# Log weights of key block 0 in stick-breaking attention: a sum over all key blocks, corrected by a triangle

## The chip, the cores and the metric

The kernel runs on one core of one Trainium2 chip. The metric is the device time of one execution in microseconds (us), and 0.2% of it is 3.8 us. The engines are named as the profile names them: PE is TensorE (PEld its weight loads), DVE is VectorE, ACT is ScalarE, POOL is GpSimd and SP is SyncE, which issues the loads.

## The reference, cut to what matters

Two transformer blocks are computed on 512 rows plus 16 meta rows, width 1024. Only the stick-breaking attention of the first block concerns this change: 16 heads of width 64.

```python
z = jnp.einsum('bhtd,bhsd->bhts', q_blk, k_pre) * scale
valid = (s_pos[None, :] < t_pos[:, None]) & (s_pos[None, :] >= PAD)
log_not = jnp.where(valid, jax.nn.log_sigmoid(-z), 0.0)
after = lax.cumsum(log_not, axis=3, reverse=True) - log_not
a = jnp.where(valid, jnp.exp(jax.nn.log_sigmoid(z) + after), 0.0)
outs.append(jnp.einsum('bhts,bhse->bhte', a, v_pre))
```

With sp = softplus(z) the log of a weight is z minus the sum of sp over this key and all later keys that the query may see. So each head needs, for each key, a reversed running sum of sp over the keys.

## The kernel before

**Tiling.** Scores are held transposed: keys on the 128 partitions, queries along the columns. The 512 keys are four key blocks. Block 0 is seen by all 512 queries, block 1 by the last 384, block 2 by 256, block 3 by 128; they are packed in `sp` at the columns `KEY_OFF`, 1280 in all. In PSUM block 0 fills bank 4, block 1 bank 5, blocks 2 and 3 share bank 6. Bank 7 holds the scores of the meta keys. Every fp32 product is made of split values: an x_hi in fp32r and the rest x_lo, so that a running sum over sp is two matmuls, one with `sp_hi` and one with `sp_lo`.

**One head** (its number is g, four heads to a quad, two heads to a pair p):

- `scores` on PE writes z into banks 4 to 6.
- `softplus` on ACT and DVE makes sp: Abs, Exp, Ln on ACT, then the maximum is added on DVE (steps sp1, sp2, sp0), ACT writes `sp_hi` (hi1 for blocks 1 to 3, hi0 for block 0), DVE `sp_lo` (sp_lo1, sp_lo0). Then DVE adds blocks 1 to 3 onto block 0, one after another, in place (L1507, steps all1 to all3): `sp[:, 0:SEQ]` is then the sum of all blocks.
- `logs` on PE subtracts the running sums from z in PSUM, by a product with a constant matrix from `cmat`: `C_TRI` (minus one on and below the diagonal) for a block onto itself, `C_ALL` (all minus one) for a later block onto an earlier one. It goes by the target block 1, 2, 3 and then 0. `logs1` is signalled after block 3, `logs0` after block 0.
- `weights` on ACT and DVE: ACT writes `sp_all_hi` (all_hi) from the sum of all blocks, DVE `sp_all_lo` (all_lo, L1512); then ACT takes Exp of the logs (a_part1, a_part2, a_part0) and the hi parts, DVE the lo parts `a_lo`.
- `meta_logs` on PE uses `sp_all_hi` and `sp_all_lo` for the meta keys, one product pair for each head, after `meta_softplus` has prepared them for both heads of the pair.
- `outputs` on PE multiplies the weights with the values.

**What sets the order.** There is no scheduler. Each engine has its own list of instructions, written by hand in a function `quad_body` per engine, and the engines meet at semaphores: `Steps` gives each step of a head a count, in the fixed order of its list. Each queue runs in order, so an instruction that waits holds all behind it. On PE the steps of one head are laced with strips of projections, which are to cover ACT and DVE: `logs(g)` stands behind the first value strip, `logs(g + 1)` behind a key strip, `logs(g + 2)` behind half of a projection, `logs(g + 3)` behind the next key strip. In quads 2 to 4 the half before `logs(g + 2)` is four strips of a "D" unit, whose results DVE adds into `acc` (L1589); strips 6 and 7 of these are added by DVE inside `softplus(g + 2)`, between sp_lo0 and the adds of L1507. In the first quad DVE copies one strip into `logit` (L1605) at that place. A strip's PSUM bank is used again two strips later, once DVE has signalled `strip_free`. In the last quad no key strip follows, and a shorter projection stands before `logs(g + 3)`.

ACT and DVE also split each 2048-column unit of weights (`split_hi`, `split_lo`), which stand in their lists between these steps.

Of the kernel before, what the change touches and what calls it, by code (L numbers as in the profile page):

```python
# [34 lines left out]
SEQ = 512  # L35
# [4 lines left out]
MROWS = 4 * META  # L40
# [131 lines left out]
def build(nc, units, xfm, meta2, consts, dec, vecs, out):  # L172
# [355 lines left out]
    def _(pe):  # L528
# [146 lines left out]

        def logs(g):

            for b in (1, 2, 3, 0):
                pe.wait_ge(hd_dve.sem, hd_dve.at("sp_lo1" if b else "sp_lo0", g))
                for b2 in range(b, BLOCKS):  # L680
                    c0 = KEY_COL[b] + P * (b2 - b)
                    for x in (sp_hi, sp_lo):
                        m = nc.tensor.matmul(psum[:, 4 + KEY_BANK[b], c0:c0 + KEY_LEN[b2]],  # L683
                                             cmat[:, C_TRI if b2 == b else C_ALL, :],
                                             x[:, KEY_OFF[b2]:KEY_OFF[b2] + KEY_LEN[b2]],
                                             start=False, stop=False, skip_group_check=True)
                if b in (3, 0):
                    m.then_inc(*hd_pe.step("logs1" if b else "logs0"))

        def meta_scores(t, p):  # L690

# [4 lines left out]
        def meta_logs(r, p, g):  # L696

            if r == 0:
                pe.wait_ge(mk_dve.sem, mk_dve.at("m_lo", p))
                for x in (m_hi, m_lo):  # L700
                    nc.tensor.matmul(psum[0:MROWS, 7, :], cmat[:, C_TRI_META, 0:MROWS], x[:, :], start=False,
                                     stop=False, skip_group_check=True)
            pe.wait_ge(hd_dve.sem, hd_dve.at("all_lo", g))
            for x in (sp_all_hi, sp_all_lo):
                m = nc.tensor.matmul(psum[0:MROWS, 7, :], cmat[:, C_ROWS + r, 0:MROWS], x[:, :], start=False,
                                     stop=False, skip_group_check=True)
            if r == 1:
                m.then_inc(*mk_pe.step("m_rows"))
# [250 lines left out]
    def _(act):  # L959
        def a(out_, in_, f, **kw):  # L960
            return nc.scalar.activation(out_, in_, f, **kw)  # L961
# [82 lines left out]
                act.wait_ge(hd_dve.sem, hd_dve.at(ready, g))  # L1044
                a(sp_hi[:, cols], sp[:, cols], ACT.Copy).then_inc(*hd_act.step(f"hi{n}"))

        def weights(g):

            act.wait_ge(hd_dve.sem, hd_dve.at("all3", g))
            a(sp_all_hi[:, :], sp[:, 0:SEQ], ACT.Copy).then_inc(*hd_act.step("all_hi"))  # L1050
            for half, cols, parts in ((1, H1, (1, 2)), (0, H0, (0,))):
                act.wait_ge(hd_pe.sem, hd_pe.at(f"logs{half}", g))
                for n in parts:
                    bank, off, w = PARTS[n]
                    a(a_f[:, off:off + w], psum[:, 4 + bank, 0:w], ACT.Exp).then_inc(*hd_act.step(f"a_part{n}"))
                act.wait_ge(hd_act.sem, hd_act.at(f"a_part{parts[-1]}", g))
                a(a_hi[:, cols], a_f[:, cols], ACT.Copy).then_inc(*hd_act.step(f"a_hi{half}"))

        def meta_softplus(p):
            act.wait_ge(mk_pe.sem, mk_pe.at("m_scores", p))  # L1060
            a(m_f[0:MROWS, :], psum[0:MROWS, 7, :], ACT.Abs).then_inc(*mk_act.step("m_abs"))
            act.wait_ge(mk_act.sem, mk_act.at("m_abs", p))
            a(m_f[0:MROWS, :], m_f[0:MROWS, :], ACT.Exp, scale=-1.0).then_inc(*mk_act.step("m_exp"))
            act.wait_ge(mk_act.sem, mk_act.at("m_exp", p))
            a(m_f[0:MROWS, :], m_f[0:MROWS, :], ACT.Ln, bias=g_col("one", 0)[0:MROWS]).then_inc(*mk_act.step("m_ln"))
            act.wait_ge(mk_dve.sem, mk_dve.at("m_sp", p))
            a(m_hi[0:MROWS, :], m_f[0:MROWS, :], ACT.Copy).then_inc(*mk_act.step("m_hi"))

# [31 lines left out]
        def quad_body(at, i, has_d, has_next):  # L1100
            g, p = 4 * i, 2 * i
            nj, ns = 3, 12 if has_d else 6
            softplus(g)
            meta_softplus(p)
            if has_d:
                y_hi(1, p - 1)
            value_hi(at, 0)
            weights(g)
            value_hi(at, 1)
            split_hi(at, 0)  # L1110
            softplus(g + 1)
            key_hi(1, at, 2, p + 1)
            weights(g + 1)
            query_hi(1, at, 3)
            meta_weights(p)
            softplus(g + 2)
            split_hi(at, 1)
            meta_softplus(p + 1)
            weights(g + 2)
            strips(at, ns - 1)  # L1120
            split_hi(at, 2)
            y_hi(0, p)
            softplus(g + 3)
# [285 lines left out]
    def _(dve):  # L1409
# [97 lines left out]
                v.tensor_tensor(sp[:, b * P:SEQ], sp[:, b * P:SEQ], sp[:, KEY_OFF[b]:KEY_OFF[b] + KEY_LEN[b]],  # L1507
                                ALU.add).then_inc(*hd_dve.step(f"all{b}"))

        def weights(g):  # L1510
            dve.wait_ge(hd_act.sem, hd_act.at("all_hi", g))
            v.tensor_tensor(sp_all_lo[:, :], sp[:, 0:SEQ], as_f32(sp_all_hi[:, :]), ALU.subtract)\  # L1512
                .then_inc(*hd_dve.step("all_lo"))
            for half, cols in ((1, slice(SEQ, PACKED)), (0, slice(0, SEQ))):
                dve.wait_ge(hd_act.sem, hd_act.at(f"a_hi{half}", g))
                v.tensor_tensor(a_lo[:, cols], a_f[:, cols], as_f32(a_hi[:, cols]), ALU.subtract)\
                    .then_inc(*hd_dve.step(f"a_lo{half}"))

        def meta_softplus(p):
            dve.wait_ge(mk_act.sem, mk_act.at("m_ln", p))  # L1520
            stt(m_f[0:MROWS, :], psum[0:MROWS, 7, :], 0.0, m_f[0:MROWS, :], ALU.max, ALU.add).then_inc(*mk_dve.step("m_sp"))
            dve.wait_ge(mk_act.sem, mk_act.at("m_hi", p))
            v.tensor_tensor(m_lo[0:MROWS, :], m_f[0:MROWS, :], as_f32(m_hi[0:MROWS, :]), ALU.subtract).then_inc(*mk_dve.step("m_lo"))

# [74 lines left out]
        def quad_body(at, i, has_d, has_next):  # L1599
            g, p = 4 * i, 2 * i  # L1600
            nj, ns = 3, 12 if has_d else 6

            def take_logit(n, s):
                strips(at, s)
                v.tensor_copy(logit[:, n, :], strip_view(at.bank(s), SEQ)).then_inc(strip_free, 1)  # L1605
            softplus(g)
            meta_softplus(p)
            if has_d:
                y_lo(1, p - 1)
            value_lo(at, 0, i)  # L1610
            weights(g)
            value_lo(at, 1, i)
            split_lo(at, 0)
            softplus(g + 1)
            key_lo(1, at, 2, p + 1)
            weights(g + 1)
            query_lo(1, at, 3, p + 1)
            meta_weights(p)
            y_take(p)
            softplus(g + 2, has_d and (lambda: add_up(acc, at, 4, range(2))),  # L1620
                     (lambda: add_up(acc, at, 6, range(2, 4))) if has_d else (lambda: take_logit(0, 4)))
            meta_softplus(p + 1)
# [433 lines left out]
def constants():  # L2058
# [10 lines left out]
    cm[:, C_BLOCKED] = np.where(i[:, None] < i[None, :], 0.0, BLOCKED)  # L2069
    cm[:, C_TRI] = np.where(i[:, None] >= i[None, :], -1.0, 0.0)  # L2070
    cm[:, C_ALL] = -1.0
    same = (i[:, None] < 2 * META) & (head[:, None] == head[None, :])
    cm[:, C_TRI_META] = np.where(same & (i[:, None] % META >= i[None, :] % META), -1.0, 0.0)
    for j in range(2):
        cm[:, C_ROWS + j] = np.where(head[None, :] == j, -1.0, 0.0)
# [100 lines left out]
```

## Time and profile before

| what | value |
|---|---|
| median of 3 runs | 1903.82 us (1903.22 to 1905.71) |
| the profiled execution | 1905.67 us, span in the trace 1903.9 us |
| PE busy | 1852.1 us, 97% |
| DVE busy, ACT busy | 1115.6 us, 731.1 us |
| the chain that ended last | PE 87%, DVE 6%, ACT 3% |
| the four quads | about 35 to 366 us of the span |

The page gives busy times and the chain that ended last. A timeline lists the instructions of an engine in order of time with start and duration. A matmul's duration holds its way through the array, so that consecutive matmuls overlap in it: what one costs PE is the distance between two starts. An idle note in brackets stands where the engine had nothing running, and names what ended it.

### The profile page before, as it was taken

To read this page: it belongs to the slowest core of one execution; us is meant where nothing else is said; L and a number is where in the kernel's file an instruction comes from. 1 tells how busy PE (TensorE), PEld (TensorE's weight loads), DVE (VectorE), ACT (ScalarE), POOL (GpSimd) and SP (SyncE) were. 2 spreads that over 40 slices of the span, in tenths; PEclk is the share of its full clock that TensorE was granted. 3 is DMA by queue.
4 is the path that set the end of the run, shared out by engine and by line. 5 is a ranking of instruction groups with operands and counts; after the bars stand their busy time and mean duration, and the time that the engine had idled before them with its cause. 6 is when DMAs were issued, how large, how long until landed. Compare 5 with 4: busy or idle time off the path is not lost.

```text
span 1903.9 us, 24558 instructions
## 1 busy us (share of the span) xinstructions
PE 1852.1 (97%) x9844; PEld 1585.1 (83%) x9844; DVE 1115.6 (59%) x1423; ACT 731.1 (38%) x868; POOL 32.6 (2%) x32
## 2 busy tenths in 40 slices
PE   9999999999999999999899999999999899999996
PEld 8898989789898888988788888886997688888885
DVE  6567566653635537356565454547688565454546
ACT  5666666433323332333342222224445542222222
POOL 2000000010000000000000000000000000000000
PEclk9999999999999999999999999999999899999998
DMA  4011111132122221112413223222467212322221
GB/s 180 28 69 60 44 44 45 45 122 78 67 88 77 88 99 66 67 67 74 195 45 108 91 88 108 90 90 87 111 177 181 108 45 89 109 89 90 108 90 45
DMA packets 24770, 168.98 MB, mean 89 GB/s; under 512 B 2688, under 2 KB 2944, under 8 KB 5248
## 3 DMA queue, kind: packets, MB, share of 16 engines
q1 hardware_dynamic: 23120, 156.51, 23.1%
q0 software_dynamic: 1584, 11.54, 2.9%
q8 instruction: 48, 0.79, 0.2%
q14 instruction: 18, 0.15, 0.0%
HBM read 154.40 MB, written 2.10 MB: 82 GB/s over the span
## 4 chain that ended last, share of the span: by engine, by line
PE 87%; DVE 6%; ACT 3%; issue 2%; DMA 1%; SPq 0%; DVEq 0%; ACTq 0%; POOL 0%; POOLq 0%
PE psum L531 28%; PE psum L532 27%; PE psum L533 27%; PE psum L683 2%; ACT w_hi L961 1%; PE psum L640 1%; DVE normed L1422 1%; DMA w_raw<-in_units 1%; DVE h L1449 1%; PE psum L611 1%; DVE w_lo L1416 1%; PE psum L593 0%; DVE normed L1466 0%; PE psum L601 0%; ACT std L961 0%
## 5 line engine op out<-in xcount | busy, mean ns | idle before, releaser
L531 PE MATMUL psum<-X_hi,w_hi 128*128 128x512 f32 (+1 forms) x1632 | 588.3, 360 | 3.1 <-DVE w_lo L1416 2.2
L532 PE MATMUL psum<-X_lo,w_hi 128*128 128x512 f32 (+1 forms) x1632 | 581.9, 357 | 0.0
L533 PE MATMUL psum<-X_hi,w_lo 128*128 128x512 f32 (+1 forms) x1632 | 581.9, 357 | 0.0
L961 ACT ACTIVATE w_hi<-w_raw 128x2048 fp32r<-128x2048 f32 x134 | 255.8, 1909 | 372.0 <-PE psum L533 364.7
L1416 DVE TENSOR_TENSOR w_lo<-w_raw,w_hi 128x2048 fp32r<-128x2048 f32 x123 | 281.7, 2290 | 135.5 <-ACT w_hi L961 135.5
L531 PEld LDWEIGHTS psum<-X_hi,w_hi 128*128 128x128 f32 x1632 | 306.8, 188 | 51.6 <-issue 4.2
L532 PEld LDWEIGHTS psum<-X_lo,w_hi 128*128 128x128 f32 x1632 | 307.4, 188 | 46.0 <-issue 2.4
L533 PEld LDWEIGHTS psum<-X_hi,w_lo 128*128 128x128 f32 x1632 | 307.0, 188 | 44.2
L1589 DVE TENSOR_TENSOR acc<-acc,psum 128x512 f32<-128x512 f32 x216 | 141.9, 684 | 59.9 <-PE psum L533 59.5
L531 PE MATMUL psum<-M_hi,w_hi 128*128 128x512 f32 x352 | 136.9, 389 | 0.0
L532 PE MATMUL psum<-M_lo,w_hi 128*128 128x512 f32 x352 | 136.9, 389 | 0.0
L533 PE MATMUL psum<-M_hi,w_lo 128*128 128x512 f32 x352 | 136.9, 389 | 0.0
L531 PE MATMUL psum<-w_hi,X_hi 128*128 128x256 f32 x384 | 108.8, 283 | 0.0
L532 PE MATMUL psum<-w_lo,X_hi 128*128 128x256 f32 x384 | 108.7, 283 | 0.0
L533 PE MATMUL psum<-w_hi,X_lo 128*128 128x256 f32 x384 | 108.6, 283 | 0.0
L1870 DVE TENSOR_TENSOR gate_in<-psum,std 128x512 f32<-128x512 f32 x44 | 30.2, 691 | 122.1 <-PE psum L533 109.0
L961 ACT ACTIVATE silu_a<-gate_in 128x512 f32<-128x512 f32 x44 | 27.6, 631 | 168.9 <-DVE gate_in L1870 168.9
L1422 DVE SCALAR_TENSOR_TENSOR z<-glu,vec,z 128x512 f32<-128x512 f32 x120 | 80.3, 746 | 0.0
L533 PEld LDWEIGHTS psum<-M_hi,w_lo 128*128 128x128 f32 x352 | 66.1, 188 | 13.7
L531 PEld LDWEIGHTS psum<-M_hi,w_hi 128*128 128x128 f32 x352 | 66.1, 188 | 13.7
L532 PEld LDWEIGHTS psum<-M_lo,w_hi 128*128 128x128 f32 x352 | 66.1, 188 | 13.7
L531 PEld LDWEIGHTS psum<-w_hi,X_hi 128*128 128x128 f32 x384 | 73.6, 192 | 0.9
(282 smaller groups left out, 2644.2 us busy)
## 6 DMA issues: line engine op xcount, KB each, us to landing
w_raw<-in_units SPq DMA_DIRECT2D x140, 1024.0 KB, 4.8
w_lo<-w_raw POOLq DMA_DIRECT2D x11, 1024.0 KB, 6.9
h<-in_xfm SPq DMA_DIRECT2D x4, 528.0 KB, 6.2
h<-in_xfm SPq DMA_DIRECT2D x1, 2112.0 KB, 7.4
decay<-in_dec SPq DMA_DIRECT2D x4, 512.0 KB, 4.4
out<-h SPq DMA_DIRECT2D x4, 512.0 KB, 2.8
rot<-in_consts SPq DMA_DIRECT2D x1, 528.0 KB, 12.3
acc<-in_consts SPq DMA_DIRECT2D x1, 448.0 KB, 10.0
```

What stands on the lines that cost most here:

```text
L531: nc.tensor.matmul(dst, w2[0], x2[0], start=first, stop=False, skip_group_check=True)
L532: nc.tensor.matmul(dst, w2[0], x2[1], start=False, stop=False, skip_group_check=True)
L533: m = nc.tensor.matmul(dst, w2[1], x2[0], start=False, stop=last, skip_group_check=True)
L611: nc.tensor.matmul(psum[:, bank, 0:P], ones[:, :], ones[:, :], start=True, stop=True)
L640: m = nc.tensor.matmul(psum[0:rows, at.bank(s) + 1, 0:256], XM[:, k, meta], y[:, k, :], start=k == 0 and y is w[0], stop=k == DT - 1 and y ...
L683: m = nc.tensor.matmul(psum[:, 4 + KEY_BANK[b], c0:c0 + KEY_LEN[b2]], cmat[:, C_TRI if b2 == b else C_ALL, :], x[:, KEY_OFF[b2]:KEY_OFF[b2 ...
L961: return nc.scalar.activation(out_, in_, f, **kw)
L1416: v.tensor_tensor(lo, w_raw[at.ring(j)][:, :], as_f32(hi), ALU.subtract).then_inc(w_lo_ready, 1)
L1422: return v.scalar_tensor_tensor(out=out_, in0=in0, scalar=scalar, in1=in1, op0=op0, op1=op1)
L1449: v.tensor_tensor(h[:, k, META:FULL], h[:, k, META:FULL], normed[:, k % 2, 0:SEQ], ALU.add)\
L1589: v.tensor_tensor(dst[:, m, :], dst[:, m, :], strip_view(at.bank(s + n), SEQ), ALU.add)\
L1870: v.tensor_tensor(gate_in[:, c, :], strip_view(at.bank(s + c), SEQ), std[:, 0:SEQ], ALU.mult)\
```

## The change

Four things are done.

1. `logs(g)` on PE first makes the blocks 1 to 3 as before. For block 0 it then makes, in place of four pairs of matmuls (512, 384, 256 and 128 columns), two pairs of 512 columns: `C_ABOVE` (one above the diagonal, else zero) with `sp_hi`, `sp_lo` of block 0, and `C_ALL` (minus one everywhere) with `sp_all_hi`, `sp_all_lo`. Minus all of block 0 plus what lies above the diagonal is the triangle; the later blocks are in the sum. The second pair waits for all_lo.
2. all_hi leaves ACT's `weights` and becomes `added_hi`; all_lo leaves DVE's `weights` and becomes `added_lo`. In the heads g + 1 and g + 3 they are called right behind `softplus`, before `key_hi` and `key_lo`. In the heads g and g + 2 they are called inside `meta_softplus`: on ACT between m_ln and m_hi, on DVE between m_sp and m_lo.
3. On ACT `meta_softplus(p + 1)` is moved ahead of `split_hi(at, 1)`.
4. The two 64-column matrices `C_ROWS` share one slot of `cmat`, which makes room for `C_ABOVE`.

The diff, cut:

```diff
         def logs(g):
-            for b in (1, 2, 3, 0):
-                pe.wait_ge(hd_dve.sem, hd_dve.at("sp_lo1" if b else "sp_lo0", g))
+            pe.wait_ge(hd_dve.sem, hd_dve.at("sp_lo1", g))
+            for b in range(1, BLOCKS):
                 for b2 in range(b, BLOCKS):
...
-                if b in (3, 0):
-                    m.then_inc(*hd_pe.step("logs1" if b else "logs0"))
+            m.then_inc(*hd_pe.step("logs1"))
+
+            pe.wait_ge(hd_dve.sem, hd_dve.at("sp_lo0", g))
+            for x in (sp_hi, sp_lo):
+                nc.tensor.matmul(psum[:, 4, :], cmat[:, C_ABOVE, :], x[:, 0:SEQ], start=False, stop=False,
+                                 skip_group_check=True)
+            pe.wait_ge(hd_dve.sem, hd_dve.at("all_lo", g))
+            for x in (sp_all_hi, sp_all_lo):
+                m = nc.tensor.matmul(psum[:, 4, :], cmat[:, C_ALL, :], x[:, :], start=False, stop=False,
+                                     skip_group_check=True)
+            m.then_inc(*hd_pe.step("logs0"))
...
-        def weights(g):
-
+        def added_hi(g):
             act.wait_ge(hd_dve.sem, hd_dve.at("all3", g))
             a(sp_all_hi[:, :], sp[:, 0:SEQ], ACT.Copy).then_inc(*hd_act.step("all_hi"))
+
+        def weights(g):
...
-        def meta_softplus(p):
+        def meta_softplus(p, then):
...
             a(m_f[0:MROWS, :], m_f[0:MROWS, :], ACT.Ln, bias=g_col("one", 0)[0:MROWS]).then_inc(*mk_act.step("m_ln"))
+            then()
             act.wait_ge(mk_dve.sem, mk_dve.at("m_sp", p))
...
             softplus(g + 2)
+            meta_softplus(p + 1, lambda: added_hi(g + 2))
             split_hi(at, 1)
-            meta_softplus(p + 1)
             weights(g + 2)
...
-        def weights(g):
+        def added_lo(g):
             dve.wait_ge(hd_act.sem, hd_act.at("all_hi", g))
             v.tensor_tensor(sp_all_lo[:, :], sp[:, 0:SEQ], as_f32(sp_all_hi[:, :]), ALU.subtract)\
                 .then_inc(*hd_dve.step("all_lo"))
```

In the loop of the quads, head g + 2, on DVE before: the second of the adds of strips 6 and 7 (`acc`), the three adds of all blocks (`sp<-sp`), the meta part, strips 8 and 9, a unit of weights, and only then `sp_all_lo`.

```order
L1589 TENSOR_TENSOR acc<-acc,psum 128x512
L1506 ISA
L1507 TENSOR_TENSOR sp<-sp 128x384
...
L1507 TENSOR_TENSOR sp<-sp 128x128
L1520 ISA
L1422 SCALAR_TENSOR_TENSOR m_f<-psum,m_f 64x512
L1522 REGISTER_ALU
L1523 TENSOR_TENSOR m_lo<-m_f,m_hi 64x512
...
L1416 TENSOR_TENSOR w_lo<-w_raw,w_hi 128x2048
L1511 REGISTER_ALU
L1512 TENSOR_TENSOR sp_all_lo<-sp,sp_all_hi 128x512
```

The same place on DVE after the change:

```order
L1605 TENSOR_TENSOR acc<-acc,psum 128x512
L1519 ISA
L1520 TENSOR_TENSOR sp<-sp 128x384
...
L1520 TENSOR_TENSOR sp<-sp 128x128
L1535 ISA
L1435 SCALAR_TENSOR_TENSOR m_f<-psum,m_f 64x512
L1524 REGISTER_ALU
L1525 TENSOR_TENSOR sp_all_lo<-sp,sp_all_hi 128x512
L1538 REGISTER_ALU
L1539 TENSOR_TENSOR m_lo<-m_f,m_hi 64x512
```

`sp_all_lo` moved ahead of `m_lo`, of two strip additions and of the unit's `w_lo`; the two strip additions and the three adds still stand before it.

On ACT, at the same head of the first quad (`w_hi` is `split_hi`, the first `a_f` is a_part1), before:

```order
L961 ACTIVATE sp_hi<-sp 128x512
L961 ACTIVATE w_hi<-w_raw 128x2048
L961 ACTIVATE m_f<-psum 64x512
L961 ACTIVATE m_f<-m_f 64x512
L961 ACTIVATE m_f<-m_f,vec 64x512
L961 ACTIVATE m_hi<-m_f 64x512
L961 ACTIVATE sp_all_hi<-sp 128x512
L961 ACTIVATE a_f<-psum 128x384 x2
```

and after:

```order
L970 ACTIVATE sp_hi<-sp 128x512
L970 ACTIVATE m_f<-psum 64x512
L970 ACTIVATE m_f<-m_f 64x512
L970 ACTIVATE m_f<-m_f,vec 64x512
L970 ACTIVATE sp_all_hi<-sp 128x512
L970 ACTIVATE m_hi<-m_f 64x512
L970 ACTIVATE w_hi<-w_raw 128x2048
L970 ACTIVATE a_f<-psum 128x384 x2
```

The unit's `w_hi` moved from the front of the meta part to its end, and `sp_all_hi` ahead of `m_hi`.

## Rows read from the trace of the kernel before

**Rows 1.** Page, part 1: busy us, share of the span, instructions.

```profile
PE 1852.1 (97%) x9844; PEld 1585.1 (83%) x9844; DVE 1115.6 (59%) x1423; ACT 731.1 (38%) x868; POOL 32.6 (2%) x32
```

**Rows 2.** PE waits, 28 to 375 us: total us, times, longest.

```profile
...
PE psum L531 <- DVE Q_lo L1422: 2.4, 1, 2.4
...
```

**Rows 3.** Timeline (start, duration us, instruction, idle): PE, head g+2, second quad.

```profile
169.62 0.45 PE L683 MATMUL psum<-sp_hi,cmat 128*128 128x512 f32 x1
...
170.89 0.45 PE L531 MATMUL psum<-Y_hi,w_hi 128*128 128x512 f32 x1
...
173.49 0.39 PE L533 MATMUL psum<-Y_hi,w_lo 128*128 128x512 f32 x1
174.01 0.50 PE L531 MATMUL psum<-Y_hi,w_hi 128*128 128x512 f32 x1
...
176.90 0.40 PE L701 MATMUL psum<-m_hi,cmat 128*64 128x512 f32 x1
...
177.46 0.45 PE L705 MATMUL psum<-sp_all_hi,cmat 128*64 128x512 f32 x1
...
177.99 0.39 PE L531 MATMUL psum<-Q_hi,K_hi 128*128 128x512 f32 x1
```

**Rows 4.** Timeline, DVE, same head (xN: N instructions merged).

```profile
168.55 1.28 DVE L1589 TENSOR_TENSOR acc<-acc,psum 128x512 f32<-128x512 f32 x2
169.74 1.33 DVE L1507 TENSOR_TENSOR sp<-sp 128x384 f32<-128x384 f32 x3
171.29 0.68 DVE L1422 SCALAR_TENSOR_TENSOR m_f<-psum,m_f 64x512 f32<-64x512 f32 x1 [0.22 <-ACT m_f L961]
...
176.72 0.69 DVE L1512 TENSOR_TENSOR sp_all_lo<-sp,sp_all_hi 128x512 fp32r<-128x512 f32 x1
```

**Rows 5.** Timeline, ACT, the same head.

```profile
167.46 1.90 ACT L961 ACTIVATE w_hi<-w_raw 128x2048 fp32r<-128x2048 f32 x1
169.26 0.57 ACT L961 ACTIVATE m_f<-psum 64x512 f32<-64x512 f32 x1
...
170.53 0.72 ACT L961 ACTIVATE m_f<-m_f,vec 64x512 f32<-64x512 f32 x1
...
172.54 0.61 ACT L961 ACTIVATE sp_all_hi<-sp 128x512 fp32r<-128x512 f32 x1
```

**Rows 6.** Timeline, head g+2 of the first quad, DVE and PE.

```profile
86.38 1.33 DVE L1507 TENSOR_TENSOR sp<-sp 128x384 f32<-128x384 f32 x3
...
88.28 0.45 PE L531 MATMUL psum<-X_hi,w_hi 128*128 128x512 f32 x1
```

**Rows 7.** Timeline, head g+1 of the second quad, DVE and PE.

```profile
146.57 1.35 DVE L1507 TENSOR_TENSOR sp<-sp 128x384 f32<-128x384 f32 x3
...
148.63 0.44 PE L683 MATMUL psum<-sp_hi,cmat 128*128 128x512 f32 x1
...
149.90 0.45 PE L531 MATMUL psum<-X_hi,w_hi 128*128 128x512 f32 x1
```

**Rows 8.** Timeline, head g of the first quad, DVE and PE.

```profile
44.37 1.34 DVE L1507 TENSOR_TENSOR sp<-sp 128x384 f32<-128x384 f32 x3
...
46.88 0.44 PE L683 MATMUL psum<-sp_hi,cmat 128*128 128x512 f32 x1
```

**Rows 9.** Timeline, head g+3 of the last quad, DVE and PE.

```profile
355.97 0.69 DVE L1512 TENSOR_TENSOR sp_all_lo<-sp,sp_all_hi 128x512 fp32r<-128x512 f32 x1
...
356.87 0.45 PE L531 MATMUL psum<-X_hi,w_hi 128*128 128x512 f32 x1
```

**Rows 10.** Timeline, PE, first product after the quads.

```profile
369.64 0.80 PE L531 MATMUL psum<-Y_hi,w_hi 128*128 128x512 f32 x1 [3.58 <-DVE Y_lo L1538]
...
374.92 0.40 PE L531 MATMUL psum<-Y_hi,w_hi 128*128 128x512 f32 x1
```

**Rows 11.** Windows: us, busy PE PEld DVE ACT POOL, PEclk, DMA share, GB/s.

```profile
33.00:36.00 3.00, 1.21 (x6) 1.10 (x7) 2.78 (x6) 2.40 (x2) 2.71 (x6) 1.00 0.79 295
...
369.00:372.00 3.00, 2.36 (x6) 1.89 (x7) 0.58 (x1) 0.00 (x0) 0.00 (x0) 0.50 0.00 0
```

More of the change, by code:

```diff
@@ L704, in meta_logs @@
             for x in (sp_all_hi, sp_all_lo):
-                m = nc.tensor.matmul(psum[0:MROWS, 7, :], cmat[:, C_ROWS + r, 0:MROWS], x[:, :], start=False,
+                m = nc.tensor.matmul(psum[0:MROWS, 7, :], cmat[:, C_ROWS, MROWS * r:MROWS * (r + 1)], x[:, :], start=False,
                                      stop=False, skip_group_check=True)
@@ L1103, in quad_body @@
             softplus(g)
-            meta_softplus(p)
+            meta_softplus(p, lambda: added_hi(g))
             if has_d:
@@ L1111, in quad_body @@
             softplus(g + 1)
+            added_hi(g + 1)
             key_hi(1, at, 2, p + 1)
@@ L1123, in quad_body @@
             softplus(g + 3)
+            added_hi(g + 3)
             if has_next:
@@ L1513, in weights @@
                 .then_inc(*hd_dve.step("all_lo"))
+        def weights(g):
             for half, cols in ((1, slice(SEQ, PACKED)), (0, slice(0, SEQ))):
@@ L1517, in weights, with meta_softplus @@
                     .then_inc(*hd_dve.step(f"a_lo{half}"))
-        def meta_softplus(p):
+        def meta_softplus(p, then):
             dve.wait_ge(mk_act.sem, mk_act.at("m_ln", p))
             stt(m_f[0:MROWS, :], psum[0:MROWS, 7, :], 0.0, m_f[0:MROWS, :], ALU.max, ALU.add).then_inc(*mk_dve.step("m_sp"))
+            then()
             dve.wait_ge(mk_act.sem, mk_act.at("m_hi", p))
@@ L1606, in quad_body @@
             softplus(g)
-            meta_softplus(p)
+            meta_softplus(p, lambda: added_lo(g))
             if has_d:
@@ L1614, in quad_body @@
             softplus(g + 1)
+            added_lo(g + 1)
             key_lo(1, at, 2, p + 1)
@@ L1621, in quad_body @@
                      (lambda: add_up(acc, at, 6, range(2, 4))) if has_d else (lambda: take_logit(0, 4)))
-            meta_softplus(p + 1)
+            meta_softplus(p + 1, lambda: added_lo(g + 2))
             if has_d:
@@ L1633, in quad_body @@
             softplus(g + 3)
+            added_lo(g + 3)
             if has_next:
@@ L2040, in z_done @@
     return 2 * TAPS_B * (t // 2) + 2 * TAPS_B - 1 + t % 2
-C_IDENT, C_BLOCKED, C_TRI, C_ALL, C_TRI_META, C_ROWS = 0, 1, 2, 3, 4, 5
+C_IDENT, C_BLOCKED, C_TRI, C_ALL, C_TRI_META, C_ROWS, C_ABOVE = range(7)
 N_CMAT = 7
@@ L2071, in constants @@
     cm[:, C_ALL] = -1.0
+    cm[:, C_ABOVE] = np.where(i[:, None] >= i[None, :], 0.0, 1.0)
     same = (i[:, None] < 2 * META) & (head[:, None] == head[None, :])
@@ L2074, in constants @@
     for j in range(2):
-        cm[:, C_ROWS + j] = np.where(head[None, :] == j, -1.0, 0.0)
+        cm[:, C_ROWS, MROWS * j:MROWS * (j + 1)] = np.where(head[None, 0:MROWS] == j, -1.0, 0.0)
     consts = np.concatenate([cos, sin, cm.reshape(P, -1)], axis=1).astype(np.float32)
```

## The prediction

> **What bounds the kernel now.** The first view is the page's busy time of the engines: PE works for 97% of the span [rows 1], so a microsecond taken from PE is won only if nothing else becomes late, and one microsecond in which PE stands still is lost whole. The next is the timeline of PE inside the quads. The reader is to see there the distance between two starts: from 170.89 to 173.49 eleven matmuls of 512 columns start [rows 3], 0.236 us each. Then the timelines of DVE and ACT around the same head tell when the sum of all blocks is there, since PE is to wait for it now. PE, DVE and ACT are all laid out by hand, so each of the four places of `logs` in a quad is looked at by itself.
>
> **What the change saves on PE.** Before, block 0 took from 169.62 to 170.89 [rows 3], 1.27 us for 2560 columns; the heads in other places show the same 1.27 (148.63 to 149.90) [rows 7]. After, it is two pairs of 512 columns, each pair behind a wait. The pair behind a wait that the trace has is that of L705: 177.46 to 177.99, 0.53 us [rows 3]. Two such pairs are 1.06 us, so a head saves 0.21 us if PE never stands, and sixteen heads 3.4 us.
>
> **What the new wait costs.** The sum of all blocks needs, behind the third add of L1507: all_hi on ACT, 0.61 us [rows 5], and all_lo on DVE, 0.69 us [rows 4]. A hand-over costs about 0.05 us: PE started at 177.46, all_lo had ended at 176.72 + 0.69 = 177.41 [rows 3, 4]. I take 0.05 for each of the three hand-overs. So PE can start the second pair 0.05 + 0.61 + 0.05 + 0.69 + 0.05 = 1.45 us after the third add ends. Now place by place.
>
> *Head g.* In the first quad the adds end at 44.37 + 1.34 = 45.71, so all_lo reaches PE at 47.16; the first pair runs from 46.88 to 47.41 [rows 8]. There is 0.25 us to spare, since a whole value strip stood in between. The later quads have more, their value strip being no shorter. Net -0.21 us, four times: -0.8 us. Behind it, m_hi on ACT moves back by almost nothing, because it waits for m_sp anyway.
>
> *Head g + 1.* The adds end at 146.57 + 1.35 = 147.92, PE may go on at 149.37; the first pair ends at 148.63 + 0.53 = 149.16. PE stands 0.21 us, and then needs 0.53 us: 149.90, which is the very time at which the next strip started before [rows 7]. The saving is eaten: 0.0 us, in all four quads. On ACT `key_hi` now stands behind all_hi, and on DVE `key_lo` behind all_lo, but their keys are needed only after another half projection and the outputs of a head; that hides it, and without this cover it would cost the 0.6 us (all_hi) by which they move.
>
> *Head g + 3* has the same order in quads 1 to 3, so again 0.0 us. In the last quad PE comes there sooner, because a projection of 512 columns stands in place of the key strip of 528. all_lo ended at 355.97 + 0.69 = 356.66 already as early as it can; PE goes on at 356.71 and is through at 357.24, against 356.87 before [rows 9]: +0.4 us.
>
> *Head g + 2* is where the sum stands or falls. On DVE the adds of L1507 stand behind two strip additions, which begin at 168.55 and end at 169.83; the three adds then end at 169.74 + 1.33 = 171.07 [rows 4]. PE may start the second pair at 172.52. But its first pair is through at 169.62 + 0.53 = 170.15 [rows 3]: PE stands 2.4 us. m_sp does not make it worse: on ACT the meta steps took from 169.26 to 171.25, 1.99 us, and moved ahead of the unit's `w_hi` they run from 167.46 to 169.45 [rows 5], so m_sp (0.68) follows the third add directly and ends about when all_hi does [rows 4]. PE is through at 173.05, against 170.89: +2.16 us.
>
> Two small waits of before then go. Strip 10 waited for its bank, since DVE came late to strip 8: 173.49 to 174.01 is 0.52 where 0.236 is usual, and the restart shows 0.50 for 0.39, together 0.39 us [rows 3]. With PE 2.2 us later, DVE is ahead of it again. And L705 waited for all_lo: the two pairs from 176.90 to 177.99 took 0.56 + 0.53 where four starts of 0.236 are 0.94, 0.15 us [rows 3]. So +2.16 - 0.39 - 0.15 = +1.6 us for quads 2, 3 and 4. What is queued behind: on ACT the unit's `w_hi` (1.90 us) now runs after m_hi, about 172.4 to 174.3, so a_part1 starts some 1.2 us later than before, at 173.15 [rows 5]; on DVE the strip additions and the unit's `w_lo` follow PE. All their users on PE stand 1.6 us or more later, so they meet the same cover. The load that SP issues behind this unit slips by about 2 us; its data are used two heads later.
>
> In the first quad only one strip copy stands there and the adds end at 86.38 + 1.33 = 87.71; PE goes on at 89.16 and is through at 89.69, against 88.28 before [rows 6]: +1.4 us, with no small waits to win back.
>
> **The sum.** Head g: -0.8. Heads g + 1 and g + 3: 0.0 and +0.4. Head g + 2: 1.4 + 3 x 1.6 = +6.2. Together +5.8 us. The profiled execution has a span of 1903.9 us and a device time of 1905.67, 1.8 us more; it becomes 1909.7 and 1911.5. The median of the runs is 1903.82, and I forecast 1903.8 + 5.8 = 1909.6 us, 0.3% slower.
>
> **Bounds.** The hand-overs are the softest term: at 0.03 in place of 0.05 each of twelve or so stalls is 0.06 shorter, -0.7 us; at 0.08 it is 0.09 longer, +1.1. After the last quad PE idles 3.58 us anyway, and then runs at half its clock: twelve matmuls from 369.64 to 374.92 took 5.28 us where 2.83 is usual, 2.45 us lost [rows 10]. How long that stretch is depends on the moment at which the clock changes, and the times of before differ among themselves by as much, 1903.22 to 1905.71. A shift of the whole program can move this by some 1.5 us in either direction.
>
> **The rivals.**
>
> *The cold clock.* PE stands 2.4 us at four places. Against this rival: a wait of 2.4 us for Q_lo near 35 us [rows 2] left the clock at 1.00 in the stretch around it; for it: after 3.58 us of idle time it was at 0.50, 1.2 GHz [rows 10, 11]. If it fell at one to four of these places, each would cost the 2.45 us of above: 1912 to 1919 us. The Trainium skill (TensorE: Matmul & The Clock Gate, "What's actually happening") states that the fast clock is held by activity and that an idle TensorE is taken back to half; by that rule the change would be worse than my sum, and the trace agrees for the long wait, not for the one of 2.4 us.
>
> *The other side: the sum is there in time.* If all_lo reached PE before it had finished the first pair, in all sixteen heads, only the saving were left: 3.4 us of PE time and three times the 0.15, 1903.8 - 3.9 = 1899.9 us, faster. It speaks for it that heads g do just this. It decides at head g + 2: the chain there must become 2.4 us shorter for the full gain, and 1.4 us shorter for no change. I see nothing that shortens it: DVE's queue has the strip additions ahead of the adds, and these wait for strips which PE finishes right before `logs`.
>
> *Only half of it shows.* The stalls come as computed, but the cold stretch behind the quads, or those around the norms, fall more favourably by up to 2.45 us, and the hand-overs are at their lower end: 1909.6 - 2.45 - 0.7 = 1906.4 us, which is inside 0.2% of before.
>
> *A later step goes late:* weights or scores of head g + 3 wait for ACT because `w_hi` moved. The cover there is the scores that PE does in between; without any of it, the 1.2 us by which a_part1 moves would be paid in three quads, 1909.6 + 3.6 = 1913.2 us.
>
> **How the numbers follow.** The forecast of 1909.6 with its own bounds (1907.7 to 1912) has 0.68; the half effect 0.14; the cold clock 0.09; the late step 0.04; the sum in time 0.05. What a measurement of this kernel can tell from no change is about 0.2%, 3.8 us. Faster by more than that is the rival in time, 0.05. Within it lie the half effect and a little of the forecast's lower edge, 0.17. Slower: 0.78. For eight times in ten the range runs from 1906.2, the half effect's end, to 1912.5, which leaves out the cold clock and the rival in time.
>
> **What would show it.** In the timeline of PE, L695 must start some 2.4 us after L691 is through at head g + 2 of every quad (about 2.0 us idle in the first, 2.2 in the others), 0.2 us after it at g + 1 and g + 3, with no idle note at g. The waits of PE must name `sp_all_lo` with some 9 us in total, and the waits for L1512 before L705 must be gone. The distance from `logs(g)` of quad 2 to that of quad 3 must grow by 1.6 - 0.2 = 1.4 us. If the chain of DVE and ACT behind the third add is much longer or shorter than 1.45 us, the size is wrong; if PEclk falls inside the quads, the first rival is right; if L695 never waits at g + 2, the forecast is wrong as a whole.

## The result, and the profile after

The changed kernel takes 1912.35 us in the median of 7 runs (1911.53 to 1917.93), the kernel before 1905.34 in as many (1903.22 to 1906.67). The ratio is 1.0041, with a 95% interval of 1.0032 to 1.0050: slower by some 7 to 8 us, where 5.8 had been forecast. The profiled execution has a span of 1910.0 us, 6.1 more than before.

PE does less work, as it should: 1849.8 us busy with 64 instructions fewer, against 1852.1 us [rows 1]. From part 1 of the page of the changed kernel:

```profile
PE 1849.8 (97%) x9780; PEld 1579.1 (83%) x9780; DVE 1115.4 (58%) x1423; ACT 730.8 (38%) x868; POOL 32.6 (2%) x32
```

What it waits for from 28 to 382 us (total us, times, longest) has a new first line, the wait of the second pair (L695) for the lower part of the sum of all blocks:

```profile
PE psum L695 <- DVE sp_all_lo L1525: 8.5, 5, 2.2
PE psum L531 <- DVE Y_lo L1554: 3.6, 1, 3.6
```

The place is head g + 2. PE in the second quad, in the changed kernel (L691 is the triangle pair, L695 the pair with the sum):

```profile
169.72 0.44 PE L691 MATMUL psum<-sp_hi,cmat 128*128 128x512 f32 x1
170.00 0.40 PE L691 MATMUL psum<-sp_lo,cmat 128*128 128x512 f32 x1
172.60 0.76 PE L695 MATMUL psum<-sp_all_hi,cmat 128*128 128x512 f32 x1 [2.20 <-DVE sp_all_lo L1525]
173.16 0.63 PE L695 MATMUL psum<-sp_all_lo,cmat 128*128 128x512 f32 x1
173.58 0.63 PE L531 MATMUL psum<-Y_hi,w_hi 128*128 128x512 f32 x1
...
175.29 0.63 PE L532 MATMUL psum<-Y_lo,w_hi 128*128 128x512 f32 x1
175.72 0.57 PE L533 MATMUL psum<-Y_hi,w_lo 128*128 128x512 f32 x1
176.12 0.40 PE L531 MATMUL psum<-Y_hi,w_hi 128*128 128x512 f32 x1
```

The idle time of 2.20 us is what was forecast, and so is the chain that causes it. The same instruction in quads 1, 3 and 4:

```profile
88.33 0.50 PE L695 MATMUL psum<-sp_all_hi,cmat 128*128 128x512 f32 x1 [1.46 <-DVE sp_all_lo L1525]
258.52 0.80 PE L695 MATMUL psum<-sp_all_hi,cmat 128*128 128x512 f32 x1 [2.22 <-DVE sp_all_lo L1525]
344.13 0.50 PE L695 MATMUL psum<-sp_all_hi,cmat 128*128 128x512 f32 x1 [2.20 <-DVE sp_all_lo L1525]
```

The fifth wait of 8.5 us is the 0.44 us at head g + 3 of quad 4. DVE and ACT at head g + 2 of the second quad:

```profile
169.82 1.34 DVE L1520 TENSOR_TENSOR sp<-sp 128x384 f32<-128x384 f32 x3
171.07 0.68 DVE L1435 SCALAR_TENSOR_TENSOR m_f<-psum,m_f 64x512 f32<-64x512 f32 x1
171.85 0.69 DVE L1525 TENSOR_TENSOR sp_all_lo<-sp,sp_all_hi 128x512 fp32r<-128x512 f32 x1
```

```profile
171.19 0.63 ACT L970 ACTIVATE sp_all_hi<-sp 128x512 fp32r<-128x512 f32 x1 [1.66 <-DVE sp L1520]
```

From the end of the third add, 169.82 + 1.34 = 171.16, to the start of L695 at 172.60 are 1.44 us; 1.45 were computed from [rows 3 to 5]. But look at the durations behind the wait. A matmul of 512 columns lasts 0.63 us there and the next starts 0.43 us later, where 0.40 and 0.236 are usual; from 176.12 on it is usual again. The granted clock of these stretches (us, busy of PE, PEld, DVE, ACT, POOL, PEclk, DMA share, GB/s), in the changed kernel:

```profile
170.00:173.00 3.00, 0.80 (x3) 0.40 (x2) 2.83 (x6) 1.81 (x3) 0.00 (x0) 0.94 0.00 0
173.00:176.00 3.00, 3.00 (x8) 2.35 (x8) 0.14 (x1) 2.97 (x5) 0.00 (x0) 0.50 0.00 0
176.00:179.00 3.00, 3.00 (x14) 2.38 (x14) 1.97 (x3) 0.95 (x2) 0.00 (x0) 0.99 0.00 0
...
258.00:261.00 3.00, 2.48 (x6) 2.02 (x7) 1.06 (x2) 2.97 (x5) 0.00 (x0) 0.50 0.00 0
...
343.00:346.00 3.00, 1.87 (x8) 1.57 (x9) 1.57 (x3) 3.00 (x4) 0.00 (x0) 1.00 0.00 0
```

So behind the stall the clock was at 0.50, 1.2 GHz. The same happened in quad 3 (258 to 261 us). In quads 1 and 4 it stayed at 1.00; the last line is the stretch behind the stall of quad 4, equally long (2.20 us idle).

To tell place from place, the distance from the first matmul of one head's `logs` to that of the next is taken from the timelines of PE. Everything else in the program is outside of these columns.

| us from `logs` to `logs` | before | after | difference |
|---|---|---|---|
| g to g + 1, quads 1 to 4 | 20.29, 20.38, 20.38, 20.30 | 19.96, 20.02, 20.02, 19.94 | -1.4 |
| g + 1 to g + 2 | 19.83, 20.90, 20.90, 20.90 | 19.75, 20.85, 20.83, 20.86 | -0.2 |
| g + 2 to g + 3 | 19.29, 20.03, 20.03, 19.66 | 20.67, 23.21, 22.93, 21.22 | +9.0 |
| g + 3 to the next g, quads 1 to 3 | 21.94 three times | 21.88, 21.86, 21.88 | -0.2 |
| g + 3 of quad 4 to the last product | 15.48 | 15.81 | +0.3 |
| ahead of the first, and behind the last | 45.45, 1534.2 | 45.03, 1533.3 | -1.4 |

The sum is +6.1 us, the difference of the spans. The last row has none of the changed work in it. Of its 1.4 us 0.4 stand ahead of the first `logs`, and 0.8 behind the wait for Y_lo, where the stretch at 1.2 GHz was shorter this time: the first twelve matmuls took 5.28 us in the kernel before [rows 10] and 4.44 after. Profiles of the same kernel differ there too: ahead of the first `logs` e1_again below has 46.32 us where this one has 45.03. Inside the quads the change cost 7.5 us.

### The profile page after: what moved, and what is told of

It is laid out like the page before. It is cut to its first block, busy times and chain, and to the rows that moved or that the text cites. A ratio compares the mean times of both kernels' runs of the same rounds, so it can differ in the third digit from the quotient of the medians.

```text
span 1910.0 us, 24430 instructions
## 1 busy us (share of the span) xinstructions
PE 1849.8 (97%) x9780; PEld 1579.1 (83%) x9780; DVE 1115.4 (58%) x1423; ACT 730.8 (38%) x868; POOL 32.6 (2%) x32
## 4 chain that ended last, share of the span: by engine, by line
PE 83%; DVE 8%; ACT 5%; issue 3%; DMA 1%; POOL 0%; DVEq 0%; SPq 0%; ACTq 0%; POOLq 0%
PE psum L531 26%; PE psum L532 26%; PE psum L533 26%; PE psum L640 1%; ACT sp L970 1%; DVE normed L1435 1%; ACT w_hi L970 1%; DVE sp L1520 1%; DMA w_raw<-in_units 1%; DVE h L1462 1%; DVE sp_lo L1513 1%; PE psum L695 1%; DVE w_lo L1429 1%; DVE sp L1435 1%; ACT sp_hi L970 0%
```

## The experiments

The theory after this profile: the stall has its computed length, 2.2 us at head g + 2, and in some of its four places, by chance, the clock falls behind it, which costs another 1.6 us or so. The rival: the moved steps on ACT and DVE make something else late. All kernels below ran beside the kernel before, on three chips, where it took 1905.80 us (e1 to e4), 1905.59 (e5 to e8) and 1905.90 (e9 to e11); each ratio is to the kernel before on the same chip. Below, a slow stretch is one in which the granted clock is at 1.2 GHz.

**The changed kernel again**, twice (e1_again and e10_again2, on different occasions; no edit).

> The changed kernel once more, beside its variants. Theory (cold clock by chance): the stall at head g + 2 has the same length each time, 1.46 us in the first quad and 2.2 us in the others, but how many of the four are followed by a stretch at 1.2 GHz differs from run to run (two in the profiled run, 3.4 us each, about 1.6 us lost in each), so single times spread over several us, 1909 to 1918, about 7 us over before in the median. Rival (later step late): no spread beyond that of before, and the 7 us stand in places outside of head g + 2.

> The changed kernel once more, on the chip of e9_warm9 and e11_laced_filled. Theory: PE stands 2.2 us at head g + 2 of quads 2 to 4 as before, and two or three of the four places are followed by a stretch at 1.2 GHz, so about 7 us over before. Rival: no such stretch, and still 7 us.

1912.38 us (1911.29 to 1914.60) and 1912.02 us (1911.73 to 1915.04), ratios 1.0036 (1.0023 to 1.0050) and 1.0039 (1.0026 to 1.0053). From `logs(g + 2)` to `logs(g + 3)` the profile of e1_again has 22.26, 23.19, 22.94 and 21.22 us, that of e10_again2 20.68, 23.15, 22.97 and 21.26. So the first quad had a slow stretch in one of three profiles, quads 2 and 3 in all three, quad 4 in none. The single times lie in two groups, 1911.3 to 1912.4 and 1914.5 to 1917.9. The profile of e1_again, at 1914.60 us, is of the second group. Its span is 2.8 us longer than that of the first profile: 1.6 us at head g + 2 of quad 1, and 1.3 us ahead of the first `logs`, where another slow stretch stands (shown below, with the prediction). The idle times were the same in all three: 8.5 to 8.6 us in five waits. The rival falls, since the loss stands at head g + 2.

**A filler in the stall** (e2_warm). `keep_warm(n, 1)` makes n small matmuls of ones. On PE, between the two pairs of block 0:

```diff
+            keep_warm(warm, 1)
             pe.wait_ge(hd_dve.sem, hd_dve.at("all_lo", g))
...
-            logs(g + 2)
+            logs(g + 2, 16 if has_d else 10)
```

> The changed kernel with 16 small matmuls of ones (10 in the first quad) between the two pairs of block 0 at head g + 2, into a PSUM bank that is free there; they add no result. At the 0.115 us that such a one cost at the start of the kernel they fill 1.8 of the 2.4 us in which PE would stand. Theory (cold clock): the granted clock stays at 1.00 through the quads, each quad keeps its 2.2 us of delay but not the 1.6 us of a cold stretch, so this is 1 to 3 us faster than the changed kernel, about 1909.5, and its times spread no more than those of before. Rival (the 7 us are the stall and moved steps alone): the same time as the changed kernel.

1915.79 us (1912.87 to 1916.37), ratio 1.0049 (1.0036 to 1.0063): slower than e1_again, where 1 to 3 us faster had been expected. The clock did stay up in the quads, but the filler was too long. PE in the second quad of e2_warm:

```profile
171.77 0.39 PE L691 MATMUL psum<-sp_lo,cmat 128*128 128x512 f32 x1
172.00 3.73 PE L611 MATMUL psum<-ones 128*128 128x128 f32 x32
```

One fp32 matmul of ones makes two rows of 0.115 us, so sixteen are 32 rows and take 3.7 us, and 2.4 were to be filled. The distances are 21.18, 22.72, 22.75 and 22.36 us, 1.1 over what e9_warm9 shows below in quads 2 to 4. So the time of this run says nothing on the theory; what speaks for it is that no stretch in the quads was slow.

**The filler at the right length** (e9_warm9): nine and six in place of sixteen and ten.

> The changed kernel with a filler in the stall at head g + 2 as in e2_warm, but of 9 matmuls (6 in the first quad). In e2_warm each turned out as two rows of 0.115 us in the trace, 0.23 us, so that 16 took 3.7 us and reached over the stall; 9 take 2.1 us of the 2.4. Theory (cold clock): no stretch at 1.2 GHz behind the stalls, all_lo still sets the time of the second pair, and from logs(g + 2) to logs(g + 3) the quads take 20.7, 21.6, 21.6 and 21.2 us, as an undisturbed one did in the changed kernel: 1.5 to 4 us under the changed kernel beside it. Rival (the falls of the clock are not caused by these stalls): the same stretches at 1.2 GHz and the same time.

1910.29 us (1908.93 to 1910.80), ratio 1.0024 (1.0014 to 1.0034), against 1912.02 for e10_again2 beside it. The distances are 20.66, 21.63, 21.63 and 21.26 us; 20.7, 21.6, 21.6 and 21.2 had been expected. PE in the second quad and the granted clock behind it, in e9_warm9:

```profile
170.51 2.17 PE L611 MATMUL psum<-ones 128*128 128x128 f32 x18
172.89 0.50 PE L696 MATMUL psum<-sp_all_hi,cmat 128*128 128x512 f32 x1 [0.21 <-DVE sp_all_lo L1526]
173.22 0.40 PE L696 MATMUL psum<-sp_all_lo,cmat 128*128 128x512 f32 x1
173.46 0.39 PE L531 MATMUL psum<-Y_hi,w_hi 128*128 128x512 f32 x1
```

```profile
173.00:176.00 3.00, 3.00 (x13) 2.44 (x14) 1.11 (x2) 2.97 (x4) 0.00 (x0) 1.00 0.00 0
```

The second pair still starts when all_lo lands, so the delay itself is kept, and only the clock is different: 1.00 where it was 0.50. This parts the loss in two. The delay alone is 1.37 + 3 x 1.6 = 6.2 us in the four places. The slow stretches add 23.21 - 21.63 = 1.58 and 22.93 - 21.63 = 1.30 us in the profile of the changed kernel, which is 2.9 us together; in e10_again2, which ran beside e9_warm9, they add as much. The medians differ by only 1.7 us and the two spans by 1.8, because outside of the quads the profile of e9_warm9 took 1.0 us longer: 0.2 ahead of the first `logs` and 0.8 behind the wait for Y_lo. The ranges of the two kernels do not touch (to 1910.80, and from 1911.73).

**The old product at head g + 2 only** (e3_g2_old): `logs_old` is the function of before.

```diff
-            logs(g + 2)
+            logs_old(g + 2)
```

> The changed kernel, but at head g + 2 PE makes block 0 in the old way, from its own blocks, and does not wait for the sum. ACT and DVE stay in the new order. Theory: what remains is -0.8 us (heads g), 0.2 us for each head g + 1 and g + 3 as traced, +0.6 in the last quad, and -0.15 us three times: within 1 us of before, no cold stretch in the quads. Rival (the moved w_hi on ACT is what costs): still 4 us or more over before.

1902.47 us (1901.08 to 1903.41), ratio 0.9981 (0.9972 to 0.9990). The loss is gone, and the kernel is faster than before by more than had been expected. Its distances from g + 2 to g + 3 are 19.30, 19.57, 19.57 and 19.19 us, three of them 0.46 under before. The moved `w_hi` costs nothing: the rival falls.

**Only the moves on ACT and DVE** (e4_order_only): `logs_old` in all four places.

> Only the moves on ACT and DVE; PE makes the logs of block 0 in the old way in all heads. Theory: the moves cost nothing by themselves and take away the three waits of L705, so -0.5 us, no difference from before that can be told. Rival (the moves are what costs): several us over before, with PE waiting for a step that was on time.

1903.21 us (1900.68 to 1904.33), ratio 0.9986 (0.9977 to 0.9995), so 2.6 us under before, where 0.5 had been expected. The quads account for 1.4 of them: 19.59, 19.54 and 19.18 us from g + 2 to g + 3 of quads 2 to 4, where before has 20.03, 20.03 and 19.66. Strip 10 of the second quad no longer loses time with its bank. PE in e4_order_only:

```profile
173.25 0.39 PE L533 MATMUL psum<-Y_hi,w_lo 128*128 128x512 f32 x1
173.48 0.49 PE L531 MATMUL psum<-Y_hi,w_hi 128*128 128x512 f32 x1
```

The two starts are 0.23 us apart, where before has 0.52 [rows 3]. The meta steps now run ahead of `w_hi`, so DVE gets to strip 8 sooner. In the prediction these 0.39 us were won because PE came later; 0.29 of them are won by the order, stall or no stall (the restart still shows 0.49 us), and the 0.15 of L705 too, which makes the 0.44 to 0.49 us of a quad. The other 1.2 us of the median lie outside of the quads and inside the width of the interval.

**The new product at head g + 2 only** (e8_g2_only): `logs_old` at the other three.

> The new logs at head g + 2 alone; the other three heads make block 0 in the old way, with ACT and DVE in the new order. Theory: the whole loss is here, 1.4 + 3 x 1.6 us and the cold stretches, 6 to 9 us over before, no less than the changed kernel within 1 us. Rival (the loss is spread over the heads): under 4 us over before.

1912.10 us (1911.85 to 1916.01), ratio 1.0038 (1.0024 to 1.0051), 6.5 us over before: the whole loss is there. The distances are 20.68, 23.01, 21.59 and 24.08 us. This time the clock fell in quads 2 and 4, in the latter for longer, and quad 3 was spared: 21.59 is the undisturbed value of e9_warm9 within 0.04 us. The profile is that of the slowest run, 1916.01 us, so the long stretch of quad 4 is not typical of the median. The granted clock behind the stall of quad 4 in e8_g2_only:

```profile
344.00:347.00 3.00, 2.14 (x5) 1.75 (x6) 1.30 (x3) 3.00 (x5) 0.00 (x0) 0.54 0.03 5
347.00:350.00 3.00, 3.00 (x8) 2.32 (x8) 0.69 (x1) 2.19 (x4) 0.00 (x0) 0.50 0.00 0
```

So the same idle time is followed by a slow stretch at one place in one kernel and at another in the other. Whether that is chance, or follows from where in the program's time the stall falls, no run shows.

**A shorter chain** (e7_adds_first): on DVE strips 6 and 7 are added behind all_lo.

```diff
-            softplus(g + 2, has_d and (lambda: add_up(acc, at, 4, range(2))),
-                     (lambda: add_up(acc, at, 6, range(2, 4))) if has_d else (lambda: take_logit(0, 4)))
+            softplus(g + 2, has_d and (lambda: add_up(acc, at, 4, range(2))))
             meta_softplus(p + 1, lambda: added_lo(g + 2))
+            add_up(acc, at, 6, range(2, 4)) if has_d else take_logit(0, 4)
```

> The changed kernel, but on DVE the additions of strips 6 and 7 (the copy of the strip in the first quad) stand behind all_lo at head g + 2, so that the adds of all blocks follow sp_lo0 directly. Theory: the chain to all_lo is 1.2 us shorter (0.7 in the first quad), PE stands about 1.0 us in place of 2.2 at head g + 2, too short for the clock to fall; strips 8 and 9 wait a little for their banks, since strips 6 and 7 are freed later. 1905 to 1908, between before and the changed kernel. Rival: strips 8 and 9 wait as long as was won, 1910 or more.

1910.90 us (1909.72 to 1912.65), ratio 1.0028 (1.0017 to 1.0040): the expected range is missed, and the time is the rival's. PE and the granted clock in the last quad of e7_adds_first:

```profile
341.76 0.50 PE L695 MATMUL psum<-sp_all_hi,cmat 128*128 128x512 f32 x1 [1.14 <-DVE sp_all_lo L1522]
342.10 0.40 PE L695 MATMUL psum<-sp_all_lo,cmat 128*128 128x512 f32 x1
343.05 0.76 PE L531 MATMUL psum<-Y_hi,w_hi 128*128 128x512 f32 x1 [0.55 <-DVE acc L1602]
```

```profile
343.00:346.00 3.00, 2.95 (x7) 2.40 (x8) 0.52 (x2) 2.94 (x6) 0.00 (x0) 0.50 0.00 0
```

The stall is 1.14 us in place of 2.20, near the 1.0 computed, but strip 8 then waits 0.55 us for the bank that DVE frees later. The undisturbed second quad takes 21.28 us, only 0.35 under e9_warm9: of the 1.06 us by which the stall is shorter 0.7 are lost again. That is most of the rival's mechanism, though not all of what was won. The rest is the clock: quads 3 and 4, with two short waits close together, were followed by slow stretches and have 22.79 and 22.45 us, while quad 2, with the same two waits (1.15 and 0.46 us), was not.

**No wait at all** (e6_no_wait): the second pair reads `sp_hi` and `sp_lo`, which leaves the later blocks out of the sum.

```diff
-            pe.wait_ge(hd_dve.sem, hd_dve.at("all_lo", g))
-            for x in (sp_all_hi, sp_all_lo):
-                m = nc.tensor.matmul(psum[:, 4, :], cmat[:, C_ALL, :], x[:, :], start=False, stop=False,
+            for x in (sp_hi, sp_lo):
+                m = nc.tensor.matmul(psum[:, 4, :], cmat[:, C_ALL, :], x[:, 0:SEQ], start=False, stop=False,
```

> The changed kernel with the second pair of block 0 made from sp_hi and sp_lo of block 0 in place of the sum of all blocks, so that PE does not wait for all_lo; the later blocks are left out of the sum, so the logs of block 0 lack them. Theory: this is the price of the matmuls alone, 0.21 us less for a head and three waits of 0.15 gone, -3.9 us, 1901.5 where before is 1905.3. Rival (the pairs cost more than the trace of before shows): less than 2 us gained.

1899.15 us (1898.24 to 1900.62), ratio 0.9968 (0.9956 to 0.9980), 6.4 us under before. More is saved than expected. At heads g, g + 1 and g + 3 of quad 2 the distances are 20.02, 20.55 and 21.59 us, 0.35 under before each. A second pair whose wait is already met is cheap, as head g of the changed kernel shows, in the first quad:

```profile
46.98 0.40 PE L695 MATMUL psum<-sp_all_hi,cmat 128*128 128x512 f32 x1
47.22 0.39 PE L695 MATMUL psum<-sp_all_lo,cmat 128*128 128x512 f32 x1
47.44 0.28 PE L531 MATMUL psum<-w_hi,X_hi 128*128 128x256 f32 x1
```

The pair takes 0.46 us, no more than two matmuls in a row, and block 0 from 46.47 to 47.44 takes 0.97, not 1.06.

**The wait put where its data are ready** (e5_laced). The second pair leaves `logs` and becomes `logs_all`, which PE does among the matmuls of the projection behind it (`mid` calls a function ahead of the given one of the eight steps):

```diff
+        def logs_all(g):
             pe.wait_ge(hd_dve.sem, hd_dve.at("all_lo", g))
...
             logs(g)
+            logs_all(g)
...
-            unit(at, 1, 2, "P", SEQ, from_x, [1])
+            unit(at, 1, 2, "P", SEQ, from_x, [1], mid=(1, lambda: logs_all(g + 1)))
...
-                unit(at, dj, ds, "D", SEQ, y, range(4, 8))
+                unit(at, dj, ds, "D", SEQ, y, range(4, 6))
+                logs_all(g + 2)
+                unit(at, dj, ds, "D", SEQ, y, range(6, 8))
```

> The changed kernel, but on PE the pair with the sum of all blocks is taken out of logs and stands among the next projection: behind one of its eight steps at heads g + 1 and g + 3, behind strip 9 at head g + 2 (behind four of eight steps in the first quad). Theory: all_lo is there by then, PE never stands for it, and the saving of 0.2 us for a head is left, 16 x 0.21 + 0.45 = 3.9 us under before, about 1901.5 where before is 1905.3. Rival (a_part0 comes too late now, since its logs are finished later): PE waits for a_lo0 or a_part0 in front of outputs or scores, and the gain is gone or the time is above before.

1898.99 us (1898.32 to 1900.26), ratio 0.9967 (0.9955 to 0.9979): 6.6 us under before, and level with e6_no_wait, the same work without the wait. No wait for `sp_all_lo` is left, and none for a late weight has come in its place. PE behind strip 9 of the second quad in e5_laced:

```profile
171.19 0.40 PE L699 MATMUL psum<-sp_all_hi,cmat 128*128 128x512 f32 x1
171.42 0.40 PE L699 MATMUL psum<-sp_all_lo,cmat 128*128 128x512 f32 x1
171.97 0.50 PE L531 MATMUL psum<-Y_hi,w_hi 128*128 128x512 f32 x1 [0.15 <-DVE acc L1612]
```

What is left is a short wait for the bank of strip 10. Because of it head g + 2 of quads 2 to 4 gains nothing over e4_order_only: 19.59, 19.59 and 19.22 us.

**And a filler in the wait behind the last quad** (e11_laced_filled), on top of e5_laced:

```diff
+        keep_warm(14, 1)
         pe.wait_ge(y_lo_ready, 2 * QUADS)
         unit(Place("quad_end"), 0, 0, "D", SEQ, seq_of(Y_hi, Y_lo))
```

> The kernel of e5_laced with 14 matmuls of ones, 3.2 us, in the 3.6 us wait for Y_lo behind the last quad, after which every kernel here ran at 1.2 GHz. Theory (an idle PE is what lets the clock fall): that stretch is gone, 1.6 to 3.3 us less than e5_laced: about 1897 where before is 1905.6. Rival: the clock falls there all the same and the time is that of e5_laced, 1899.

1895.54 us (1894.76 to 1896.34), ratio 0.9950 (0.9937 to 0.9964), 3.5 us under e5_laced, and 3.8 when each is set against the kernel before on its own chip (10.4 and 6.6 us under). The stretch behind the wait, first in e5_laced and then in e11_laced_filled:

```profile
362.00:366.00 4.00, 1.90 (x5) 1.53 (x6) 2.04 (x2) 0.00 (x0) 0.00 (x0) 0.51 0.00 0
366.00:370.00 4.00, 4.00 (x13) 3.20 (x12) 1.31 (x2) 0.00 (x0) 0.00 (x0) 0.64 0.00 0
```

```profile
362.00:366.00 4.00, 3.54 (x19) 2.87 (x19) 1.86 (x3) 0.00 (x0) 0.00 (x0) 1.00 0.00 0
366.00:370.00 4.00, 4.00 (x19) 3.24 (x18) 2.07 (x3) 0.00 (x0) 0.00 (x0) 1.00 0.00 0
```

19 matmuls in place of 13 in the same 4 us. The first twelve behind the wait take 2.89 us, in e5_laced 5.07, so the place itself gave 2.2 us, inside the expected 1.6 to 3.3; the medians are a little over it. The profile of e11_laced_filled is 5.0 us shorter than that of e5_laced. Of the rest 0.8 us stand ahead of the first `logs` and 1.9 behind this stretch, where e5_laced has two more slow stretches, near 912 and 1308 us (granted clock 0.60 and 0.59 in 911:914 and 1307:1310), and e11_laced_filled has none at the same places of the program. The filler is not shown to be the cause of that: e4_order_only, which has no filler, has no slow stretch at the first of the two either. This kernel beats both, by 10 us against the kernel before and by about 16 against the changed one.

## Why the prediction was right and wrong

**The direction, the place and the length of the stall were right.** Slower had 0.78. Head g + 2 was named as what decides; the chain of 1.45 us measured 1.44; PE was idle 1.46, 2.20, 2.22 and 2.20 us. (The sign that named about 2.0 us idle for the first quad did not fit the prediction's own numbers: the first pair would be through at 88.28 - 1.27 + 0.53 = 87.54 and PE go on at 89.16 [rows 6], which is 1.6 us.) Without a fall of the clock the place cost 1.37 us in the first quad (1.4 forecast) and 1.60 in each of the others (1.6 forecast), as e9_warm9 shows in all four and quads 1 and 4 in the changed kernel itself.

**The step that failed is the verdict on the cold clock.** The sum held nothing for it, and as a rival it was set aside with 0.09, because a wait of 2.4 us near 35 us had left the clock at 1.00 [rows 2, 11]. That was one observation of a thing that varies. The same wait, in the profile of e1_again (stretches as above):

```profile
33.00:36.00 3.00, 1.90 (x10) 1.79 (x11) 2.79 (x5) 1.73 (x1) 2.71 (x6) 0.93 0.75 306
36.00:39.00 3.00, 3.00 (x14) 2.50 (x13) 1.06 (x1) 1.50 (x4) 2.69 (x1) 0.50 0.29 49
```

Of the thirteen profiles of this case four have a fall there (the distance from the first scores to the first `logs` is 12.2 us and not 10.65). And no profile in which PE stood at head g + 2 without a filler was spared: two places were hit in the changed kernel, e7_adds_first, e8_g2_only and e10_again2, three in e1_again. The prediction's own sign for this rival, a PEclk that falls inside the quads, came, and from `logs(g)` of quad 2 to that of quad 3 the distance grew by 2.7 us, where 1.4 had been forecast. The evidence should have been read as "sometimes", times four places. The price for a place was also off: 2.45 us had been taken from the stretch behind the 3.58 us wait [rows 10]; here 1.3 to 1.6 us were lost where the clock fell once, and 2.8 us (24.08 - 21.26) only in quad 4 of e8_g2_only. Two places at about 1.5 us are the 2.9 us by which the profile of the changed kernel exceeds e9_warm9 at head g + 2. The Trainium skill (TensorE: Matmul & The Clock Gate, "What's actually happening") says of the rise at the start of a kernel that its point varies from run to run, since the monitor's window does not start with the kernel. The thirteen profiles show a thing of the same kind for falls: the same wait is followed by 1.2 GHz in some and not in others.

**The saving of the matmuls was too small.** Both pairs of block 0 had been priced at 0.53 us, the price of a pair that waited for data [rows 3]. In the changed kernel the first pair takes 0.51 us and a second pair whose wait is met 0.46, so `logs` is 0.30 us shorter, and the head as a whole saves 0.33 to 0.36 us and not 0.21: -1.4 us at the four heads g where -0.8 was forecast, and about -0.05 at heads g + 1 and g + 3 where 0.0 was. The last quad's head g + 3 cost +0.33, for +0.4. Together 1.1 us in the kernel's favour.

**The sum.** The forecast of +5.8 with the saving put right is +4.7. In e9_warm9, which has just that and a steady clock, the distances in the quads add up to 4.8 us over before, and the medians, 1910.29 against 1905.9, to 4.4. Two places with a slow stretch add some 2 to 3 us, which makes the 7. So the two errors went in opposite directions, and the forecast was nearer to the result than its parts were. That the median of 1912.35 us lies just inside the stated range (to 1912.5) is luck too: the range was to leave out the cold clock, which is in the result, and the saving that the sum had too small made room for it.

**The small waits** (0.39 and 0.15 us in three quads) did go, 0.44 to 0.49 us for a quad, but by the order on ACT and DVE, as e4_order_only shows, and not because PE came later. For the sum of the change it is nearly the same; for a kernel without the stall it is a gain of its own, which the prediction would have missed.

**The other side's mechanism was real.** The rival said that the time from which it decides is the arrival of all_lo before PE has done the first pair. Moving the pair instead of the sum does this, and gives 6.6 us, not the 3.9 computed, for the reason above.

## What to carry to other kernels

Fewer matmuls are worth something only if their operand is there: here a product that saves a third of a microsecond waited 2.2 us at one place of four, and the cure was to move the product among work that needs nothing from it. Price a stall of TensorE twice, once as its length and once as what the clock may do behind it, and do not take one trace in which the clock held as proof that it will. Where a wait can't be avoided, matmuls that compute nothing, no longer than the wait, gave back 1.7 us by the medians in the stalls at head g + 2 (9 matmuls, 2.1 us) and 2.2 us in the wait behind the quads (14 matmuls, 3.2 us); 16 in the first place were too long and cost 1.1 us in each of quads 2 to 4.

## What the runs showed of the hardware

- The clock can fall with waits far shorter than the long one of before, which was 3.58 us: behind 2.20 and 2.22 us (the changed kernel), behind 1.46 us (e1_again, quad 1: distance 22.26 for 20.67 us), and behind 1.14 and 0.55 us with one pair of matmuls in between (e7_adds_first).
- A stall with the same idle time to 0.02 us is followed by 2.4 GHz at one place and 1.2 GHz at another of the same run. In the three profiles of the changed kernel quads 2 and 3 were hit each time and quad 4 never; quad 1 and the wait near 35 us changed, both hit in e1_again alone.
- A small fp32 matmul of ones (128x128, 128 columns) stands as two rows of 0.115 us in the trace, 0.23 us in all; whoever sizes a filler from one row makes it twice too long, as in e2_warm.
- Why quad 4 was spared in three profiles of the changed kernel, while e8_g2_only, whose other heads are a little longer, was hit there and not in quad 3, stays open: no run moved one stall alone in time.
